# GLA, retention and mLSTM outputs by queries in a one-core kernel of four decoder layers

## The reference, cut to what matters

```python
# GLA, layer 0
o = gla_attention(q, k, v, log_a)                       # (B, S, 4, 256)
o = rmsnorm(o, gla_out_norm).reshape(B, S, 1024) * silu(r)

# retention and mLSTM, both layers of the second block
def _head_norm(h, g):                                   # h: (B, S, 4, 256)
    mu = h.mean(-1, keepdims=True)
    var = square(h - mu).mean(-1, keepdims=True)
    return ((h - mu) * rsqrt(var + NORM_EPS)).reshape(B, S, 1024) * g
o_ret = _head_norm(_retention(rq, rk, rv), ret_norm_g) * silu(r_g)
y_ret = o_ret @ w_proj_ret
# in _mlstm, with qk = (q k^T) * D
den = qk.sum(-1) + ...
denom = maximum(abs(den), exp(-m_row))
h = num / denom
o_ml = _head_norm(h, mlstm_norm_g) * sigmoid(m_o)
y_ml = o_ml @ w_proj_mlstm
```

## Time and profile before

| | |
|---|---|
| median of three runs | 2063.55 us (2060.15 to 2065.45) |
| profiled execution, its own time | 2065.46 us |
| its span, first to last instruction | 2063.7 us |
| TensorE busy | 2042.7 us |
| VectorE busy | 1267.6 us |
| ScalarE busy | 1004.7 us |
| GpSimd busy | 73.3 us |
| mean granted TensorE clock | 0.995 |

### The profile page before, as it was taken

How to read it: one execution, slowest core, us unless ns; L and a number is a source line. 1 busy time by engine, 2 the same in 40 slices (tenths; PEclk the granted TensorE clock), 3 DMA queues, 4 the chain that set the end, 5 groups by cost and what they waited for, 6 DMA issues and landing times.

```text
span 2063.7 us, 37372 instructions
## 1 busy us (share of the span) xinstructions
PE 2042.7 (99%) x15928; PEld 1956.7 (95%) x15928; DVE 1267.6 (61%) x1163; ACT 1004.7 (49%) x939; POOL 73.3 (4%) x53
## 2 busy tenths in 40 slices
PE   9999999999999999999999999999999999999998
PEld 8999998999999999689999999999998999999997
DVE  6556665655575576656555665675456575676545
ACT  5545645434454457545344663644434554544333
POOL 2000000100010000000000000100000000100000
PEclk9999999999999999999999999999999999999999
DMA  7555452455555544225555444564554434465552
GB/s 299 184 183 183 164 181 105 163 185 190 195 185 191 193 165 167 99 103 213 183 183 184 164 146 162 184 245 157 189 183 164 184 143 151 177 225 184 183 183 102
DMA packets 51218, 362.32 MB, mean 176 GB/s; under 512 B 5680, under 2 KB 6832, under 8 KB 7728
## 3 DMA queue, kind: packets, MB, share of 16 engines
q1 hardware_dynamic: 49856, 353.05, 47.4%
q0 software_dynamic: 1264, 7.80, 1.1%
HBM read 359.78 MB, written 1.05 MB: 175 GB/s over the span
## 4 chain that ended last, share of the span: by engine, by line
PE 94%; DVE 3%; ACT 2%; DMA 1%; issue 1%; DVEq 0%; SPq 0%; ACTq 0%
PE ps L242 23%; PE ps L244 22%; PE ps L243 22%; PE ps L518 3%; PE ps L519 3%; PE ps L517 3%; PE ps L291 2%; PE ps L289 2%; PE ps L290 2%; PE ps L790 1%; PE ps L501 1%; PE ps L495 1%; PE ps L496 1%; DMA raw<-in_slots 1%; ACT whi L233 1%; PE ps L340 1%
## 5 line engine op out<-in xcount | busy, mean ns | idle before, releaser
L238 DVE TENSOR_TENSOR wlo<-raw,whi 128x2048 fp32r<-128x2048 f32 x325 | 755.6, 2327 | 456.5 <-ACT whi L233 455.7
L242 PE MATMUL ps<-in_hi,whi 128*128 128x256 f32 x3596 | 1016.3, 283 | 2.3 <-DVE in_lo L313 2.1
L243 PE MATMUL ps<-in_lo,whi 128*128 128x256 f32 x3596 | 1006.2, 280 | 0.0
L244 PE MATMUL ps<-in_hi,wlo 128*128 128x256 f32 x3596 | 1005.0, 279 | 0.0
L233 ACT ACTIVATE whi<-raw 128x2048 fp32r<-128x2048 f32 x325 | 619.4, 1908 | 194.2 <-PE ps L244 163.5
L242 PEld LDWEIGHTS ps<-in_hi,whi 128*128 128x128 f32 x3596 | 678.3, 189 | 11.0 <-issue 4.9
L243 PEld LDWEIGHTS ps<-in_lo,whi 128*128 128x128 f32 x3596 | 678.3, 189 | 3.2 <-issue 1.4
L244 PEld LDWEIGHTS ps<-in_hi,wlo 128*128 128x128 f32 x3596 | 678.1, 189 | 0.0
L242 PE MATMUL ps<-h_hi,whi 128*128 128x256 f32 x480 | 134.5, 280 | 0.0
L243 PE MATMUL ps<-h_lo,whi 128*128 128x256 f32 x480 | 133.9, 279 | 0.0
L244 PE MATMUL ps<-h_hi,wlo 128*128 128x256 f32 x480 | 133.9, 279 | 0.0
(11 more groups left out here) (296 smaller groups left out, 2153.9 us busy)
## 6 DMA issues: line engine op xcount, KB each, us to landing
raw<-in_slots SPq DMA_DIRECT2D x333, 1024.0 KB, 4.8
ws<-in_lngb POOLq DMA_DIRECT2D x4, 1024.0 KB, 5.0
ws<-in_mem_t POOLq DMA_DIRECT2D x2, 1024.0 KB, 10.0
consts<-in_consts SPq DMA_DIRECT2D x1, 1600.0 KB, 14.5
consts<-in_consts POOLq DMA_DIRECT2D x1, 1472.0 KB, 6.7
x<-in_x_t SPq DMA_DIRECT2D x1, 1024.0 KB, 7.7
y<-x SPq DMA_DIRECT2D x1, 512.0 KB, 2.6
y<-x SPq DMA_DIRECT2D x2, 256.0 KB, 2.1
```

Of the source, the lines that this page charges most:

```text
L238: dve.tensor_tensor(wlo[:, j], raw[:, j], whi[:, j].bitcast(F32), ALU.subtract).then_inc(lo_ready, 1)
L242: pe.matmul(out, whi[:, j, o:o + n], hi, start=start, stop=False, skip_group_check=True)
L243: pe.matmul(out, whi[:, j, o:o + n], lo, start=False, stop=False, skip_group_check=True)
L244: return pe.matmul(out, wlo[:, j, o:o + n], hi, start=False, stop=stop, skip_group_check=True)
```

## The change

**Outputs by queries.** The value products take the scores as stationary operand and the values as moving one: 12 products of 256 columns in place of 8 of 256 and 8 of 128. The output has 128 queries on partitions and the 256 features of a head along the free axis.

**Norms along the free axis.** VectorE takes the statistics of each of the 8 pieces (2 query tiles by 4 heads) with `bn_stats` and `bn_aggr`, straight from PSUM. For GLA the mean square is mean squared plus variance; ScalarE makes the reciprocal root, and VectorE multiplies output, factor and gate in one instruction. For the other two ScalarE normalises out of PSUM with scale and bias per partition, and VectorE multiplies by the gate. The products with ones, the GpSimd additions, the centring, the squares and the wide factors are gone.

**Turn back.** TensorE transposes the gated result (16 transposes of 128x128 for each of the three) into PSUM, and the split into high and low part reads from there and applies the gain, which is per partition again.

**Gates by tokens.** The slots of the GLA gate `r`, of the retention gate and of the mLSTM output gate are computed by tokens.

**One-column sums.** Behind each value product of mLSTM stands one with the same stationary operand and one column of ones, into 8 columns of PSUM. The denominators and their reciprocal are 128 x 8. The exponentials of the row maxima are turned to tokens by two more small products, and the broadcast carries 256 columns a head in place of 512.

**Order.** In the GLA stage the first turn comes before the memory scores and the second behind them, the first two output slots are done in two halves each by output features, and output slot 3 comes behind the attention product. In the second block the two turns stand between the last merge-gate slots and behind the first slot of the retention projection.

The core of the diff:

```diff
+        def head_out(t, h):
+            return ps[:, 2 * t + h // 2, (h % 2) * 256:(h % 2 + 1) * 256]
+        def pe_values2(pe, v, sums=None):
+            def both(t, h, w, first, done, tk):
+                last = pe.matmul(head_out(t, h), w, v[:, tk, h * 256:(h + 1) * 256], start=first, stop=done, ...)
+                if sums is not None:
+                    last = pe.matmul(sums(t, h), w, ones[:, 0:1], start=first, stop=done, ...)
             for h in range(HEADS):
-                for d in range(2):
-                    ...
+                both(0, h, scores2[:, h, P:2 * P], True, True, 0)
+                both(1, h, scores2[:, h, 2 * P:384], True, False, 0)
+                both(1, h, scores2[:, h, 0:P], False, True, 1)
+        def dve_head_stats(dve, n, rd=None):
+            for t in range(2):
+                for h in range(HEADS):
+                    last = dve.bn_stats(hn_parts[:, 4 * t + h], head_out(t, h))
+            ...
+            for g in range(8):
+                last = dve.bn_aggr(hn_mv[:, g], hn_parts[:, g])
+            (copy of the variance, or twice its product with rd)
+        def act_head_r(act, n):            # wait hn_var; Ln, Exp of 128 x 8
+        def dve_head_shift(dve, n, rd=None):  # wait hn_r; one or two products of 128 x 8
+        def act_head_norm(act, n, out):
+            act.wait_ge(hn_shift, 2 * n + 2)
+            for t in range(2):
+                for h in range(HEADS):
+                    g = 4 * t + h
+                    last = act.activation(out[:, t, h * 256:(h + 1) * 256], head_out(t, h), ACT.Identity,
+                                          scale=hn_scale[:, g:g + 1], bias=hn_bias[:, g:g + 1])
+        def pe_head_turn(pe, n, src):      # 16 transposes into banks 0-3 or 4-7
+        def act_head_hi(act, n, gain, k0, m, at):  # high part out of PSUM, scale=gain(k)
+        def dve_head_lo(dve, n, sp, gain, k0, m, at):  # low part out of PSUM
 layer2_pe
-            run(S_MQK + 1, S_MQK + 3)
-            pe_head_sums(pe, n, "mean")
-            run(S_MQK + 3, S_MV)
-            run(S_MV, S_MV + 2, True)
-            pe_head_sums(pe, n, "var")
-            run(S_MV + 2, S_RG, True)
-            pe.wait_ge(cen_act, CA("factor", n))
+            run(S_MQK + 1, S_MV)
+            run(S_MV, S_RG, True)
+            pe.wait_ge(hn_done, n + 1)
 (broadcast: rows ROW_M:ROW_E + 1, 512 columns -> ROW_M, 256 columns)
-            run(S_RG, S_RG + 3)
+            run(S_RG, S_RG + 3, True)
             (scores)
-            run(S_RG + 3, S_MO)
+            run(S_RG + 3, S_MO + 1, True)
             pe.wait_ge(ml_dve, LD("scores", l))
-            (8 products of ones with the scores)
-            run(S_MO, S_MO + 2)
-            pe.wait_ge(ml_dve, LD("denom", l))
-            pe_values2(pe, l_v).then_inc(ml_pe, 1)
-            run(S_MO + 2, S_GA + 3)
-            pe_head_sums(pe, n + 1, "mean")
-            run(S_GA + 3, S_GB + 2)
-            pe_head_sums(pe, n + 1, "var")
+            pe_values2(pe, l_v, lambda t, h: den[:, 4 * t + h:4 * t + h + 1]).then_inc(ml_pe, 1)
+            run(S_MO + 1, S_GA, True)
+            run(S_GA, S_GB + 2)
+            pe.wait_ge(ret_dve, TD("gated", l))
+            pe.wait_ge(hn_done, n + 2)
+            pe_head_turn(pe, n, r_o)
             run(S_GB + 2, B2_RET - B2)
+            (after the first slot of the retention projection: pe_head_turn(pe, n + 1, l_o))
 layer2_act
             copy(S_MQK + 3, l_qk[:, 6:8])
-            act_head_square(act, n, r_o)
+            act_log_exp(act)
+            act_head_r(act, n)
             values(S_MV, l_v, 0)
+            act_head_norm(act, n, r_o)
             values(S_MV + 1, l_v, 1)
...
             merge_gate(S_GA, gate_a, 0)
+            act_log_exp(act)
+            act_head_r(act, n + 1)
+            hi(S_GA + 1)
+            act_head_norm(act, n + 1, l_o)
 pe_gla
+            turn_out(0)
             (memory scores)
+            turn_out(1)
+            clear(0), clear(2), out(0, (0, 1, 4, 5)), out(1, (0, 1, 4, 5))
+            clear(1), clear(3), out(0, (2, 3, 6, 7)), out(1, (2, 3, 6, 7))
+            pe_turn(pe, 0, 4, g_probs)
             pe_out(pe, L0_OUT, 2, GLA_OUT_AT)
+            pe_attend(pe, 0, 4, g_probs_t, ...)
             pe_out(pe, L0_OUT, 3, GLA_OUT_AT)
```

More of the change, by code:

```diff
@@ new lines, in out_lo @@
+            def out_lo(g):
+                dve.wait_ge(split_hi, SPLIT_GLA + 1 + 2 * g)
+                for d in range(2):
+                    last = dve.scalar_tensor_tensor(gla_places(in_lo, g, d), gla_turned(g, d), par("gla_out", d),
+                                                    gla_places(in_hi, g, d).bitcast(F32), ALU.mult, ALU.subtract)
+                last.then_inc(split_lo, 1 + g)
+            dve.wait_ge(gla_rstd, 1)
+            gated(0)
+            gated(1).then_inc(gla_dve, 1)
@@ L1698, in pe_head_sums @@
[L1698 to L1703, removed]
-        def dve_head_centre(dve, n, src):
-            dve.wait_ge(cen_pe, CP("mean", n))
-            for h in range(HEADS):
-                v = src[:, 2 * h:2 * h + 2]
-                last = dve.scalar_tensor_tensor(v, bcast(head_mean[:, h], 2), -1.0 / 256, v, ALU.mult, ALU.add)
-            last.then_inc(cen_dve, 1)
@@ new lines, in pe_head_turn @@
+        def pe_head_turn(pe, n, src):
+            for k in range(DT):
+                for t in range(2):
+                    last = pe.transpose(head_turned(n, k)[:, t * P:(t + 1) * P], src[:, t, k * P:(k + 1) * P], ident)
+                if k % 4 == 3:
+                    last.then_inc(hn_turned, 1)
+        def act_head_hi(act, n, gain, k0, m, at):
+            act.wait_ge(hn_turned, 2 * n + 1 + k0 // 4)
+            for k in range(k0, k0 + m):
+                last = act.activation(in_hi[:, at + k - k0], head_turned(n, k), ACT.Copy, scale=gain(k))
+            last.then_inc(split_hi, 1)
@@ L1731, in build @@
+        def dve_head_lo(dve, n, sp, gain, k0, m, at):
+            dve.wait_ge(split_hi, sp + 1)
+            for k in range(k0, k0 + m):
+                last = dve.scalar_tensor_tensor(in_lo[:, at + k - k0], head_turned(n, k), gain(k),
+                                                in_hi[:, at + k - k0].bitcast(F32), ALU.mult, ALU.subtract)
+            last.then_inc(split_lo, 1)
         LN_SUMS = 12
@@ L1852, in layer2_pe @@
-            run(S_MV + 2, S_RG, True)
-            pe.wait_ge(cen_act, CA("factor", n))
+            for i, row in enumerate((ROW_A, ROW_E)):
+                for t in range(2):
+                    o = 256 + 8 * i + 4 * t
+                    last = pe.matmul(ps[:, 7, o:o + 4], rows[0:4, row, t * P:(t + 1) * P], ident[0:4, 0:4],
+                                     start=True, stop=True, skip_group_check=True)
+            last.then_inc(ml_pe, 1)
+            run(S_MQK + 1, S_MV)
+            run(S_MV, S_RG, True)
@@ L2197, in layer2_dve @@
-            last.then_inc(ret_dve, 1)
-            dve.wait_ge(ret_dve, TD("gated", l))
-            dve.wait_ge(ml_pe, LP_("out", l))
-            dve.wait_ge(ml_dve, LD("recip3", l))
-            for h in range(HEADS):
-                last = dve.tensor_tensor(l_o[:, 2 * h:2 * h + 2], pair(ps[:, h, :]), bcast(l_rd[:, h * T:(h + 1) * T], 2), ALU.mult)
-            last.then_inc(ml_dve, 1)
+            dve.reciprocal(l_rd[:, :], l_rd[:, :]).then_inc(ml_dve, 1)
+            dve.wait_ge(ml_dve, LD("recip", l))
```

368 lines of the change are left out of this document (194 added, 174 removed).

## The result

The kernel after takes 2046.08 us (median of four runs, 2044.72 to 2046.61), the kernel before 2064.5 beside it (2060.15 to 2065.74): a ratio of 0.9906 (0.9893 to 0.9919), 0.9% faster. The forecast was 2046.2.

A forecast was written before the change was run, and what follows sets the result against it. TensorE, busy 2042.7 of 2063.7 us, was taken as the bound, so its queue's changes count one for one. -7.75 - 2 x 5.3 + 2 x 0.5 = -17.4 us gave a median of 2046.2 us, range 2041.5 to 2052.5.

The forecast's parts named there:

- GLA, -7.75: GLA stage: products with ones, waits and slow scores go, transposes and slots by tokens are added; sum -7.75 us.
- The wait for the silu: GLA stage: TensorE's wait for the last gate slot's silu goes, as ScalarE has nothing from VectorE ahead; -3.1 us.
- the 1.8 us of half clock: GLA stage: the memory scores, at clock 0.50 behind the wait, run at 1.00 instead; -1.8 us.
- Each layer, -4.8 with the stall: Each of two retention/mLSTM layers: terms sum to -5.3 us, with a stall of 0.5 added back.
- the one-column products: mLSTM, each layer: twelve added products, 24 records at 0.133 us, cost +3.2 us; bounds 1.6 and 5.2.
- The lower bound: One-column products, mLSTM: first load of each pair hides behind the 256-column product ahead, so they cost 1.6 us.
- The stall, +0.5: Each layer: TensorE waits for conversions behind the normalisation chain, retention 0.5 us (0 to 1.5), mLSTM 0 (up to 1).
- Head sums, broadcast, denominators, turns, gates: Each layer's other terms: head sums -7.0, broadcast -1.8, denominators -2.6, two turns +3.5, gate turns +0.5 us.
- The half clock behind the broadcast, -1.6: Each layer: with half the broadcast's columns the clock no longer falls behind it; -1.6 us, other end 0.
- rival A: Half the broadcast still brings the clock down in both layers, 2 x 1.6 us more: 2049.4 us; chance 0.13.
- Rivals B and E: B: normalisation chain later at four places, 2054.2 us, chance 0.11. E: GLA wait stays behind another instruction, 2051.1, chance 0.07.
- C: Normalisation chain late by a conversion round at four places, half clock behind each wait: 28.8 us, 2075; chance 0.02.

The follow-up runs named there:

- e1: The kernel before with only the GLA part of the change; ratio 0.9962, span 2055.3 us.
- e2: The kernel before with only the retention and mLSTM part of the change; ratio 0.9938, span 2052.3 us.
- e7: The kernel after with memory scores ahead of both turns in GLA and mLSTM's one-column products behind all value products; span 2050.7 us.
- e5: The kernel before, unchanged, profiled a second time; 2063.93 us, span 2062.0 us.
- e8: The kernel after with the GLA attention product behind output slot 3 and ScalarE's 8 normalisations done twice; ratio 0.9967, span 2059.1 us.
- e6: The kernel after, unchanged, profiled a second time; ratio 0.9908, span 2044.8 us.
- e10: The kernel after with the broadcast at 512 columns and each of its four products done twice; ratio 0.9994, span 2061.1 us.
- e9: The kernel after with gate turns as transposes and GpSimd adding two score tiles, leaving 8 of 12 one-column products; 2043.74 us, ratio 0.9891.

## Why the prediction came out, point by point

- **What bounds the kernel**: right. TensorE is the chain before and after, and the terms taken from its queue came off one for one, each part alone as in the whole (e1, e2).
- **GLA, -7.75**: measured -8.0. The waits and scores went as stated. Two points of its reasoning were incomplete. The wait for the silu went by ScalarE's order, but what keeps another of 2.15 us away is the first turn's place ahead of the scores (e7). And the 1.8 us of half clock are no constant of the kernel: before and e2 had it behind the wait of 2.9, but e5 ran the old GLA stage at 1.00, and the change was then worth 6.3 there. The output slot between attention and split was worth 1.7 where 1.4 was taken (e8). The turn of the probabilities (340.28 in after) waited for nothing.
- **Each layer, -4.8 with the stall**: measured -6.5. The term most wrongly sized is the one-column products: 24 x 0.108 = 2.6 us where 24 x 0.133 = 3.2 was taken, 0.6 too much. The nearest row, 4 records of 4 columns over 0.53 us, holds the passage into the next slot, and over so few records that is a fifth. The Trainium skill's rule, which the prediction set beside the row, says 2.6: by "TensorE: Matmul & The Clock Gate", section "LDWEIGHTS (loading the stationary operand)", a load takes the columns over 1.2 GHz, 0.107 us for 128, and the trace agrees at 0.108. The lower bound, that a load hides behind the product ahead, is refuted: 24 records took 24 times 0.108 between the values too.
- **The stall, +0.5**: measured 0. The retention chain had 1.5 us to spare where -0.5 was worked out. Statistics and aggregates took 3.4 us for 8 of each (4.2 taken), the normalisations 3.6 for 3.7, and of the 0.7 us for handovers next to nothing is seen. The mLSTM chain had 0.2 where 0.1 was worked out, for the first conversion behind its factors; the conversion behind its normalisations, which the prediction did not look at, had 2.3. Twice the normalisations (e8) confirmed the 1.5 and the 2.3 from the other side, and did not lengthen what stands ahead of the 0.2.
- **Head sums, broadcast, denominators, turns, gates**, each with the slower first products behind it: four head sums took 6.9 us (4 x 1.54 and some 0.7 behind them) for 7.0; the broadcast lost 1.7 for 1.8; the denominators 2.6 for 2.6; turns 3.5 for 3.5; gate turns 0.4 for 0.5. With the one-column products (+2.6) and the half clock (-1.5) that makes -6.2. The rest is the pace of the slots, followed here in the first layer. The eight slots by tokens cost 0.3 and not 0.5, because some of them had not run at the 5.60 us of the prediction's unit price before, but at 5.65. The same holds for 13 slots by features from the first merge-gate slot to the end of the stage: the slot at 1338.05 in before takes 5.65 us, the same one at 1325.44 in after 5.60. Both prices come back in e5 and e6, so they belong to the kernel and not to the execution, and they are worth 0.6 us. The prediction, which priced every slot by features alike, had put this at nothing. All terms together give the 6.5; what sets the two paces is open.
- **The half clock behind the broadcast, -1.6**: right in the pair of profiles (two falls before, none after), wrong as a statement about the kernel. By the prediction's own rows the stretch is 16 x (0.21 - 0.117) = 1.5 us and not 1.6, and 1.5 is what it measured. The clock still fell behind half the broadcast, 4 times in 12; so rival A's mechanism is real, and an estimate from the two counts makes the term worth some (0.8 - 0.33) x 1.5 = 0.7 us a layer on average. That the profiled execution of after had neither fall was in part luck: at 4 in 12, an estimate is that both places stay clear in under half of the executions. Where "TensorE: Matmul & The Clock Gate" in the Trainium skill ties the slow clock to idleness (section "What's actually happening"), e10 shows it fall with TensorE busy for 3.4 of 3.4 us, and the measurement decides.
- **What was missing**: +1.6 us in the latent attention stage, 10.2 us of half clock for 6.8. It is a matter of the execution. Over 13 profiles this stretch was 10.2 us in five, 6.8 in five and absent in three, 3.6 to 3.7 us of time between the ends. The surplus of 3.4 in the layers and 0.2 in the GLA stage and this loss of 1.6 cancel in part and leave 2.0 us between the spans and the sum. That 2046.08 met the forecast of 2046.2 within 0.1 us is luck: it was counted down from a median of 2063.55, and the kernel before then stood at 2064.5 (18.4 above after) and at 2065.56 in e6 (19.1 above).

Rivals B and E did not occur. C did not either, but e8 shows how near its mechanism is: a chain 3.8 us longer went with 7.3 us a layer, part of it half clock behind a wait.

## What to carry to other kernels

Price a small fp32 product by its two records, 0.108 us each here with one column, and much the same with 128 (0.22 to 0.23 us from one start to the next at L1866 in before), and count them before fusing or splitting a sum; adding the operands on an idle engine first removes records (e9). Before a half-clock stretch enters a sum, look at it in a second execution, and price it by how often it appears. Turning an output back with transposes is cheap against summing over partitions, if the transposes stand where they also cover the eviction and the split behind them.

## What the runs showed of the hardware that I had not expected

- The granted clock fell at different places in two executions of one program: before had half clock for 3.4, 6.8, 3.4 and 3.4 us at four places, e5 for 10.2 and 3.4 us at two.
- Before TensorE's last product, it fell in 13 profiles only at these places: behind the wait of 2.9 us in the GLA stage (2 of 3), in the latent attention stage with its waits of 0.8, 1.1 and 1.5 us (10 of 13), during or behind the 4-row broadcasts (16 of 26), behind the waits of 2.3 us of e8 (2 of 2), and behind the block of one-column products of e7 (1 of 2).
- A one-column fp32 product costs 0.22 us in either place, half of what one of 256 columns costs.
